# Hybrid decoder layer on one core: zero products on TensorE up to the first projection, tile 0's root ahead, and a different order of the last steps

## What is computed

```python
h = rmsnorm(x, attn_norm_w)                 # first norm
p = h @ w_in                                # combined projection, 9232 columns
# retention and gated delta net on parts of p, gates, two branch products
x = x + m @ w_out
x = x + moe_top4_of_32(rmsnorm(x, ffn_norm_w))   # 32 experts, each 1024 -> 2048 -> 1024
y = rmsnorm(x, final_norm_w)                # last norm: y_prompt (256 rows), y_sample (8 rows)
```

## Time and profile before

| | us |
|---|---|
| median of 3 runs | 1414.34 |
| lowest and highest of them | 1414.23, 1415.02 |
| profiled execution, its own time | 1416.62 |
| its span, from the first to the last instruction | 1414.3 |

### The profile page before, as it was taken

One profiled execution on the slowest core, in us unless ns is written; L12 is line 12 of the kernel. 1 busy time (PEld: TensorE's weight loads), 2 busy tenths in 40 slices (PEclk: granted clock), 3 DMA queues, 4 the chain that ended last, 5 costly groups with the idle time before them and its releaser, 6 DMA issues.

```text
span 1414.3 us, 17959 instructions
## 1 busy us (share of the span) xinstructions
PE 1376.6 (97%) x7571; PEld 669.2 (47%) x7571; DVE 511.7 (36%) x1090; ACT 255.6 (18%) x467; POOL 108.6 (8%) x107
## 2 busy tenths in 40 slices
PE   8999999999999999999999999999999999999996
PEld 6888885578887533333333333333323333333332
DVE  5655344313112219322432342223422234223423
ACT  3443341122200221111101110111111011011102
POOL 0102110100000001000100010001000011000100
PEclk9999999999999999999999999999999999999999
DMA  7532527554639799999999999999999999999995
GB/s 232 209 129 85 180 76 236 188 176 145 228 120 373 300 413 428 427 428 431 432 428 427 429 432 430 430 427 430 430 429 430 427 430 434 424 428 427 427 427 228
DMA packets 81807, 481.16 MB, mean 340 GB/s; under 512 B 13919, under 2 KB 34831, under 8 KB 61587
## 3 DMA queue, kind: packets, MB, share of 16 engines
q1 hardware_dynamic: 80644, 478.58, 83.1%
q10 hardware_dynamic: 986, 1.08, 0.3%
q0 software_dynamic: 96, 0.33, 0.1%
HBM read 468.85 MB, written 11.26 MB: 339 GB/s over the span
## 4 chain that ended last, share of the span: by engine, by line
PE 81%; DMA 16%; DVE 2%; issue 0%; ACT 0%; DVEq 0%; ACTq 0%
PE bank L1280 25%; PE bank L1304 12%; DMA ring<-in_w_gate_up 11%; PE bank L724 7%; PE bank L712 6%; DMA ring<-in_w_down 5%; PE bank L1252 5%; PE bank L1123 4%; PE bank L993 4%; PE bank L1334 3%; PE bank L1146 2%; DVE Ssg L2204 1%; PE bank L697 1%; PE bank L1260 1%; PE bank L1289 1%; PE bank L1344 1%
## 5 line engine op out<-in xcount | busy, mean ns | idle before, releaser
L1280 PE MATMUL bank<-ring,xT 128*64 128x512 f32 x2048 | 475.5, 602 | 12.1 <-DMA ring<-in_w_gate_up 11.1
L1280 PEld LDWEIGHTS bank<-ring,xT 128*64 128x64 f32 x2048 | 135.7, 137 | 282.5 <-issue 259.0
L2418 DVE TENSOR_TENSOR glu<-bank,bgb 128x512 f32<-128x512 f32 x32 | 22.1, 691 | 569.5 <-PE bank L1280 555.2
L1304 PE MATMUL bank<-ring,acT 128*64 128x512 f32 x992 | 218.7, 592 | 0.9 <-DMA ring<-in_w_down 0.8
L1304 PEld LDWEIGHTS bank<-ring,acT 128*64 128x64 f32 x992 | 71.1, 137 | 142.1 <-issue 140.8
L724 PE MATMUL bank<-HT,wslot 128*128 128x264 f32 x512 | 119.5, 389 | 0.0
L1918 POOL PARTITION_BROADCAST bgb<-hrow x31 | 40.8, 1317 | 979.5 <-DVE lin L2419 768.3
L724 PEld LDWEIGHTS bank<-HT,wslot 128*128 128x128 f32 x512 | 95.3, 190 | 19.7 <-issue 4.6
L712 PE MATMUL bank<-HT,wslot 128*128 128x264 f32 x384 | 89.5, 394 | 0.8 <-DVE HT L1965 0.8
L1252 PE MATMUL bank<-hrow,O 128*64 128x512 f32 x372 | 89.6, 599 | 0.0
L712 PEld LDWEIGHTS bank<-HT,wslot 128*128 128x128 f32 x384 | 73.9, 194 | 15.3 <-issue 2.3
(11 more groups left out here) (429 smaller groups left out, 1167.2 us busy)
## 6 DMA issues: line engine op xcount, KB each, us to landing
ring<-in_w_gate_up SPq DMA_DIRECT2D x44, 4096.0 KB, 26.7
ring<-in_w_down SPq DMA_DIRECT2D x62, 2048.0 KB, 25.3
ring<-in_w_gate_up SPq DMA_DIRECT2D x36, 2048.0 KB, 28.4
wslot<-in_w_in SPq DMA_DIRECT2D x17, 2048.0 KB, 8.2
ring<-in_w_gate_up SPq DMA_DIRECT2D x8, 1024.0 KB, 8.9
out<-Ssg SPq DMA_DIRECT2D x8, 512.0 KB, 5.3
Ssr<-in_state_ret SPq DMA_DIRECT2D x4, 1024.0 KB, 10.3
out<-Ssr SPq DMA_DIRECT2D x4, 1024.0 KB, 8.5
```

The costliest lines, as they stand in the source:

```text
L1280: t = pe.matmul(B[part][64 * g:64 * g + 64, :], block_of(xT, k), w[:, D * part + 512 * g:D * part + 512 * g + 512], start=(k == 0), stop=( ...
L1304: t = pe.matmul(home[64 * g:64 * g + 64, :], block_of(acts, 2 * k + a), w[:, D * a + 512 * g:D * a + 512 * g + 512], start=(k == 0 and a = ...
```

## The change

Three edits. First, PE gets products of zeros: `dq` is a tile that DVE has set to zero at the start, and `keep_clock(n)` multiplies 128 x 128 of it by 128 x 128 of it n times, into a bank that the first projection tile overwrites. Nine come ahead of the first transpose, two ahead of each of the first two diagonal products, two behind the last. Second, the root, the inverse and the diagonal of tile 0 are made on their own, ahead of those of tiles 1 and 2; the copy of the convolution weights `cw` moves on DVE from ahead of the `HT` blocks to behind them. Third, the end is done tile by tile in another order: tile 0, sample tokens, tile 1. Tile 0's root is taken as soon as its sum is there, DVE finishes tile 0 first, and tile 1 is finished half by DVE and half by ACT, with the ACT half multiplied by `WN` ahead of time into `weighted_rows` (unused ring space) and stored by ACT's own queue. The ACT engine's read of the number of extra blocks moves ahead of the last sums.

```diff
-            sp.wait_ge(s_h0, 1)
+            sp.wait_ge(s_h, 1)
             sp.dma_start(o[0][0][0:P, :], hrow[:, 0, :]).then_inc(s_fin, 16)
-            sp.wait_ge(s_h, 1)
-            sp.dma_start(o[0][0][P:2 * P, :], hrow[:, 1, :]).then_inc(s_fin, 16)
             sp.wait_ge(s_h, 2)
+            sp.dma_start(o[0][0][P:2 * P, 0:512], hrow[:, 1, 0:512]).then_inc(s_fin, 16)
+            sp.wait_ge(s_h, 3)
             for j in range(2):
                 sp.dma_start(ys[:, 256 * j:256 * j + 256], hd[32 * j:32 * j + NB, :]).then_inc(s_fin, 16)
-            sp.wait_ge(s_fin, 96)
+            sp.wait_ge(s_fin, 112)
...
         def _(pe):
+            def keep_clock(n):
+
+                for _ in range(n):
+                    pe.matmul(B[0][:, 0:P], dq[:, 0:P], dq[:, P:2 * P], start=True, stop=True)
+
+            pe.wait_ge(s_init, 1)
+            keep_clock(9)
             pe.wait_ge(s_const, 16)
             for c in (0, 2, 1):
                 r = TILES[c][1]
-            pe.wait_ge(s_dg, 1)
-            for c, r in TILES:
+            for n, c in enumerate((0, 1, 2)):
+                r = TILES[c][1]
+                if n < 2:
+                    keep_clock(2)
+                pe.wait_ge(s_dg, (1, 2, 3)[n])
                 t = pe.matmul(B[1][:, P * c:P * c + r], K[0:r, C_ONE:C_ONE + P], dg[0:r, c, 0:r], start=True, stop=True)
             t.then_inc(s_rsb, 1)
+            keep_clock(2)
...
-                for j in range(4):
-                    g, f = j // 2, 256 * (j % 2)
-                    t = pe.matmul(B[4][32 * j:32 * j + 32, 0:256], xg[64 * g:64 * g + 64, 2 * P:2 * P + 32],
-                                  yb[64 * g:64 * g + 64, f:f + 256], start=True, stop=True)
-                t.then_inc(m_cb, 1)
                 for c in range(2):
                     for g in range(2):
                         t = pe.matmul(homes[c][g][:, :], xg[64 * g:64 * g + 64, P * c:P * c + P],
                                       yb[64 * g:64 * g + 64, :], start=True, stop=True)
                     t.then_inc(m_cb, 1)
+                    for j in range(4) if c == 0 else ():
+                        g, f = j // 2, 256 * (j % 2)
+                        t = pe.matmul(B[4][32 * j:32 * j + 32, 0:256], xg[64 * g:64 * g + 64, 2 * P:2 * P + 32],
+                                      yb[64 * g:64 * g + 64, f:f + 256], start=True, stop=True)
+                    if c == 0:
+                        t.then_inc(m_cb, 1)
...
             nc.scalar.preload_act_table_set("sqrt_and_others")
-            for c in range(2):
+            for c, first, last in ((0, 0, 1), (1, 1, 3)):
                 act.wait_ge(s_x[c], 16)
                 nc.scalar.activation(sqx[:, :], xtok[:, c, :], ACT.Square, accum_out=ss[:, c:c + 1]).then_inc(s_ss, 1)
                 act.wait_ge(s_ss, c + 1)
-            act.wait_ge(s_ss2, 1)
-            nc.scalar.activation(rs[:, :], ss[:, :], ACT.Sqrt, bias=eps[:, :], scale=1.0 / D).then_inc(s_rs, 1)
+                if c == 1:
+                    act.wait_ge(s_ss2, 1)
+                nc.scalar.activation(rs[:, first:last], ss[:, first:last], ACT.Sqrt, bias=eps[:, :], scale=1.0 / D
+                                     ).then_inc(s_rs, 1)
...
-                for n, (f, scratch) in enumerate(((Xd[:, :], rest[:, 0:256]), (X[:, 0, :], rest[:, 0:D]),
-                                                  (X[:, 1, :], rest[:, D:2 * D]))):
+                for n, (f, scratch, col) in enumerate(((X[:, 0, :], rest[:, 0:D], 0), (Xd[:, :], rest[:, 0:256], 2),
+                                                       (X[:, 1, :], rest[:, D:2 * D], 1))):
                     after(act, m_acc, 3, b, n + 1 if isinstance(b, int) else 3)
                     if n == 1:
                         after(act, s_fss, 3, b, 1 - 3 * (NE - 1))
-                    if n == 2:
-                        after(act, s_fsum, 1, b, 2 - NE)
-                        nc.scalar.activation(rs[:, 2:3], B[0][:, 0:1], ACT.Sqrt, bias=eps[:, :], scale=1.0 / D
+                    nc.scalar.activation(scratch, f, ACT.Square, accum_out=ss[:, col:col + 1]).then_inc(s_fss, 1)
+                    if n == 1:
+                        nc.scalar.activation(rs[:, 0:1], ss[:, 0:1], ACT.Sqrt, bias=eps[:, :], scale=1.0 / D
                                              ).then_inc(s_frs, 1)
-                    nc.scalar.activation(scratch, f, ACT.Square, accum_out=ss[:, (n + 2) % 3:(n + 2) % 3 + 1]).then_inc(s_fss, 1)
+                after(act, s_fsum, 1, b, 2 - NE)
+                nc.scalar.activation(rs[:, 2:3], B[0][:, 0:1], ACT.Sqrt, bias=eps[:, :], scale=1.0 / D).then_inc(s_frs, 1)
                 after(act, s_fss, 3, b, 3 - 3 * (NE - 1))
-                nc.scalar.activation(rs[:, 0:2], ss[:, 0:2], ACT.Sqrt, bias=eps[:, :], scale=1.0 / D).then_inc(s_frs, 1)
-
+                nc.scalar.activation(rs[:, 1:2], ss[:, 1:2], ACT.Sqrt, bias=eps[:, :], scale=1.0 / D).then_inc(s_frs, 1)
+
+            act.wait_ge(s_ext, 2)
+            many = act.value_load(xni[0:1, 0:1], min_val=0, max_val=NEXTRA)
             norm_sums(NE - 1)
...
-            extra_blocks(act, extra)
-            act.wait_ge(s_fw, 2)
-            nc.scalar.activation(hrow[:, 0, :], X[:, 0, :], ACT.Copy, scale=rs[:, 0:1]).then_inc(s_h0, 1)
-            act.wait_ge(s_h, 2)
+            extra_blocks(act, extra, many)
+            act.wait_ge(s_hw, 1)
+            act.wait_ge(s_fw, 1)
+            link(nc.scalar.activation(hrow[:, 1, 512:D], weighted_rows, ACT.Copy, scale=rs[:, 1:2]))
+            act.dma_start(o[0][0][P:2 * P, 512:D], hrow[:, 1, 512:D]).then_inc(s_fin, 16)
+            act.wait_ge(s_h, 3)
...
-            dve.wait_ge(s_const, 16)
-            dve.wait_ge(s_rs, 1)
-            link(v.reciprocal(rs[:, :], rs[:, :]))
-            for c, r in TILES:
-                t = v.tensor_scalar(dg[0:r, c, 0:r], K[0:r, C_ID:C_ID + r], rs[0:r, c:c + 1], None, ALU.mult)
-            t.then_inc(s_dg, 1)
-            for j in range(2):
+            def prompt_columns(j):
                 dve.wait_ge(s_tr, j + 2)
                 v.tensor_copy(XT[:, 2 * j:2 * j + 2, 0:2 * P], B[2 + j][:, :].rearrange("p (k t) -> p k t", k=2)
                               ).then_inc(s_xd, 1)
+
+            def diagonal(c):
+                r = TILES[c][1]
+                v.tensor_scalar(dg[0:r, c, 0:r], K[0:r, C_ID:C_ID + r], rs[0:r, c:c + 1], None, ALU.mult).then_inc(s_dg, 1)
+            dve.wait_ge(s_const, 16)
+            dve.wait_ge(s_rs, 1)
+            link(v.reciprocal(rs[:, 0:1], rs[:, 0:1]))
+            diagonal(0)
+            dve.wait_ge(s_rs, 2)
+            link(v.reciprocal(rs[:, 1:3], rs[:, 1:3]))
+            diagonal(1)
+            diagonal(2)
+            for j in range(2):
+                prompt_columns(j)
             dve.wait_ge(s_cwT, 1)
-            v.tensor_copy(cw[:, :, :], B[7][:, 0:4 * CCH].rearrange("p (i c) -> p c i", i=4)).then_inc(s_cw, 1)
             v.tensor_copy(nw[:, :, :], B[7][:, 4 * CCH:4 * CCH + 2 * KT].rearrange("p (i k) -> p i k", i=2)
                           ).then_inc(s_cw, 1)
-            dve.wait_ge(s_cw, 2)
+            dve.wait_ge(s_cw, 1)
             dve.wait_ge(s_xd, 3)
             dve.wait_ge(s_rsb, 1)
             for k in range(KT):
@@ -1964,6 +1991,8 @@
                     dve.wait_ge(s_xt, k // 2 - 1)
                 v.scalar_tensor_tensor(HT[:, k, :], XT[:, k, :], nw[:, 0, k:k + 1], B[1][:, 0:TOK], ALU.mult, ALU.mult
                                        ).then_inc(s_ht, 1)
+            v.tensor_copy(cw[:, :, :], B[7][:, 0:4 * CCH].rearrange("p (i c) -> p c i", i=4)).then_inc(s_cw, 1)
+            dve.wait_ge(s_cw, 2)
...
-                after(dve, m_cb, 3, n, 1)
                 after(dve, m_acc, 3, n)
-                v.tensor_tensor(Xd[:, :], Xd[:, :], B[4][:, 0:256], ALU.add).then_inc(m_acc, 1)
                 for c in range(2):
-                    after(dve, m_cb, 3, n, c + 2)
+                    after(dve, m_cb, 3, n, 1 + 2 * c)
                     for g in range(2):
                         f = X[:, c, 512 * g:512 * g + 512]
                         t = v.tensor_tensor(f, f, homes[c][g][:, :], ALU.add)
                     t.then_inc(m_acc, 1)
+                    if c == 0:
+                        after(dve, m_cb, 3, n, 2)
+                        v.tensor_tensor(Xd[:, :], Xd[:, :], B[4][:, 0:256], ALU.add).then_inc(m_acc, 1)
...
             dve.wait_ge(s_wn, 80)
-            dve.wait_ge(s_fss, 2)
-            v.tensor_tensor(X[:, 0, :], X[:, 0, :], WN[:, :], ALU.mult).then_inc(s_fw, 1)
-            dve.wait_ge(s_frs, 2)
-            v.reciprocal(rs[:, :], rs[:, :]).then_inc(s_fw, 1)
-            dve.wait_ge(s_fw, 2)
-            v.scalar_tensor_tensor(hrow[:, 1, :], X[:, 1, :], rs[:, 1:2], WN[:, :], ALU.mult, ALU.mult).then_inc(s_h, 1)
+            v.tensor_tensor(weighted_rows, X[:, 1, 512:D], WN[:, 512:D], ALU.mult).then_inc(s_hw, 1)
+            dve.wait_ge(s_frs, 1)
+            link(v.reciprocal(rs[:, 0:1], rs[:, 0:1]))
```

(8 more changed lines are left out.)

11 lines of the change are left out of this document (5 added, 6 removed).

## The result

The changed kernel takes 1411.24 us (median of 22 runs, 1410.48 to 1414.06); the kernel before took 1413.85 in the same series (22 runs, 1411.25 to 1417.13). The medians differ by 2.6 us. The ratio is 0.9984 with a 95% interval of 0.9979 to 0.9990: faster by 2.3 us, between 1.4 and 3.0. The direction was as forecast, the size half of it (4.6 us). A gain under 0.2% had a chance of 0.39 in the forecast, one over 0.2% the larger one of 0.59.

What follows compares the result with a forecast made beforehand. PE was taken to bound the start up to the expert loads' restart, and the end to count in full: 3.3 us at the start (1.2 + 2.1) plus 1.3 at the end, 4.6 off 1414.3, gives 1409.7 us, range 1408.6 to 1413.4.

Steps and rivals of the forecast that it cites:

- The base: Whole kernel: 4.6 us were subtracted from the profiled span of 1414.3 us, said to stand at the runs' median, 1414.34.
- the hole: Expert loads, 484 to 488 us, DMA share 0.01, ended by PE's use of ring slots; was to come some 3.3 us earlier.
- Clock (term 2.1 us): First projection tile: zero products bring PE to full clock from about 6.5 us, so the tile's pace gains 2.1 us.
- Earlier `HT` (term 1.2 us): Start: faster transposes and diagonal products let the `HT` blocks start at 10.7 us and not 11.88, 1.2 us earlier.
- the row of factors is then ready at about 10.65 instead of 11.8: Start, ahead of `HT`: PE and DVE end together near 10.6 us, with zero products between the diagonal products.
- End (term 1.3 us): Final stores: small stores issued 0.8 to 1.8 us earlier, taken as 1.3; last root and last arithmetic unmoved.
- 2.4 us later: Kernel end: time from SP's last small-store issue, 1411.91 us, to the end at 1414.3.
- Its own signs: Wrong if second eight transposes still take 1.9 us, first tile over 5, or add-back to end (12.9) shrinks under 0.8.
- Lost to the loads: Rival: the restart of the expert loads is not PE's doing, only the end's 1.3 us stays; 1413.0 us, chance 0.07.
- As late as before: Rival: clock rises near 14 us despite the zero products, `HT` at 13.6; most likely 1412.8 us, chance 0.26.
- Falls again during the transposes: Rival: clock rises, then falls during the transposes; start gains 0.6 to 2.1 us, time 1411.2 us, chance 0.10.
- Slower: Rival: zero products delay the start at low clock and buy nothing, losing 1.8 to 3 us; 1415.8 us, chance 0.04.

Runs made afterwards that it cites:

- e1: The changed kernel without any of its zero products; measured 1413.1 us, ratio 0.9993 to the kernel before.
- e6: The changed kernel without zero products, its sixteen transposes of prompt tokens done as ordinary products with the identity; 1412.93 us, one run.
- e12: The kernel before, unchanged, profiled once more; one run, 1412.33 us, span 1410.0.
- e2: The changed kernel with only the nine zero products ahead of the first transpose, the six later ones removed; 1411.28 us, ratio 0.9984 to the kernel before.
- e5: The changed kernel with only the nine zero products ahead and the second load of constants issued second on ACT's queue; 1411.5 us, ratio 0.9985.
- e9: The changed kernel once more, without an edit, as second look and control; 1410.97 us, ratio 0.9987 to the kernel before.
- e8: The changed kernel with the sample tokens finished and stored ahead of tile 1, so that large stores go last; 1410.56 us, ratio 0.9979.
- e4: Only the end pieces of the change (add-back order, `norm_sums`, stores) put on the kernel before; 1411.91 us, ratio 0.9983.

## Why the prediction was right, and where its sizes were off

**The base.** "It stands at the median of the runs (1414.34)" was a false comparison. The forecast itself had written that the profiled execution's own time is 2.3 us longer than its span, and then set the span beside times. The own time of that execution, 1416.62, lies near the top of 22 runs (median 1413.85), and the earlier trace rows had most of the reason in it: the clock at 0.53 just where PE sets the restart, which cost 1.9 us. The forecast quoted that row for two rivals and did not take it as a cost of this execution. Subtracting its own 4.6 us from 1413.85 would have given 1409.25, further from the measured 1411.24 than 1409.7 was. That the changed kernel's span, 1409.2, came near the forecast is luck: the base held the spell. So is the hole, which was to come 3.3 us earlier and came 3.5: 2.07 from the tile and 1.9 from the spell, less the wait of 0.5.

**Clock (term 2.1 us).** Right in mechanism and in size: 5.88 to 3.80. The rise came at 4.6 to 7.8 us in all eight profiles with nine products ahead, in seven of them 0.5 to 1.9 us behind the last of the nine, and at 11.9 to 17.0 in the four with transposes alone; in the one with four products ahead it came at 12.36. That the order of the start alone moves nothing is shown by e1. That it is the kind of product that counts rests on one profile, e6, and the early rise of e12 shows how much single profiles differ. What was missed is that the kernel before is not always cold: in one profile of four the 2.1 us are not there to be gained. The Trainium skill says that the point of the rise differs between executions ("TensorE: Matmul & The Clock Gate", Part 1). The traces agree, but the page gives 500 ns either way where two profiles of one kernel here have 4.58 and 7.53, and two of the kernel before 11.93 and 16.73. The forecast held this as a rival for the changed kernel and should have applied it to the kernel before.

**Earlier `HT` (term 1.2 us).** This step failed: "the row of factors is then ready at about 10.65 instead of 11.8". It went through PE's and DVE's instructions and left out the load that the diagonal products wait for. In the kernel before that load landed at 9.07, 1.3 us ahead of its use, and so in no wait; the forecast had PE ready for it at 9.0, which left no room, and in this execution it landed at 9.78. Behind it the four zero products between the diagonals cost 0.9 us of chain (1.92 us from 9.83 to 11.75, where e2 took 1.02), which the forecast had laid beside DVE's work. e2 gives 0.6 of the term back, e5 0.9, and e9, where the load landed at 8.97, 0.8 by chance. The forecast's 0.3 us from the zeros to PE's first record was 0.06.

**End (term 1.3 us).** The order of the steps was forecast to 0.1 us (first store at 6.47 against 6.5, last root unmoved), and the last issue came 1.1 us earlier. The step that failed is the one from the issue to the end, "2.4 us later": it was 3.2 in the changed kernel. The tail went from 12.83 to 12.89 in three profiles to 12.4 to 12.6 in seven with this order and to 11.49 in one. The last packet of the large stores is 1.3 us earlier relative to the add-back (10.41 for 11.75), so their bytes do not hold it. The last packet of all is 0.9 us earlier, and 0.6 of that is lost between it and the last landing (1.12 us for 0.48). That the last landings are small stores holds it in part, as e8 took 0.6 off by order alone. Why one profile in eight had 11.49 stays open.

**Its own signs.** The forecast called itself wrong if the time from the first add-back product to the end had not shrunk by 0.8 us. It shrank by 0.3, so by this sign the end was wrong. The two others (the second eight transposes, the first tile) came out as forecast. The tile's 2.07 us and the tail's 0.3 add up to 2.4, near the measured 2.3. That is partly luck: the kernel before starts cold in some executions and warm in others, five profiles lost 0.3 to 0.5 us at 247 us, and end only was 2.4 us faster by itself.

**Rivals.** Lost to the loads: refuted by the 466.6 us from tile to restart in seven profiles, whatever the tile, and by e1 against the changed kernel (2.2 us at the tile, 1.7 at the restart). As late as before: its condition was met only with four products ahead. Falls again during the transposes: not seen in eight profiles. Slower: it took four products ahead in place of nine to see the chain that it describes (1415.79 us, one run, with a spell in it, and the first tile at full clock). Two prices do not follow from their own terms: a start gain of 0.6 to 2.1 with the end's 1.3 makes 1410.9 to 1412.4, of which the forecast took 1411.2 and not the middle, and 0.4 gained to 0.8 lost makes 1412.6 to 1413.8, where it had 1412.2 to 1413.8.

## What to carry to other kernels

A wait that the profile does not show may be the next one: before a chain is shortened, list the landings that its links wait for and how long each has been idle, not only who waits now. Work that is put in to hold the clock belongs where the engine would idle anyway; between two links of a chain it can cost its full time (0.9 us for four products here).

Before a term is subtracted from a profiled span, set that execution's own time among the other runs, and look through its clock column for stretches below 1.00.

## What the runs showed that I had not expected

The same program is read with the first tile at 5.88 and at 3.80 us: the clock's rise without extra products was at 11.93 to 16.95 us. A landing of 144 KB issued at 2.67 us varied from 8.8 to 9.9 us. From the end of the last issue of an 8 KB store to the end of the kernel it took 3.2 us in the changed kernel, 2.1 in e4, whose end is the same, and 2.4 in the kernel before.
